# A final stage whose two accumulators are added on GpSimd instead of by accumulating DMAs

## What is computed

```python
hb = silu(xb @ exp_w1[e]) * (xb @ exp_w3[e])      # a block of 128 tokens, expert e
yb = hb @ exp_w2[e]
routed = segment_sum(yb * slot_w, slot_tok)        # add every block's rows to its tokens
y = routed + shared                                # shared: one expert that takes all tokens
x = x + g2 * y                                     # g2: one row for context, one for latents
out = x * rsqrt(mean(x * x) + EPS) * norm_final
```

## Time and profile before

| | us |
|---|---|
| median of 3 runs | 2050.85 (2050.64 to 2053.70) |
| the profiled execution | 2054.07 |
| its span in the trace | 2052.3 |
| PE busy in the span | 1856.0 (90%) |
| DVE busy | 1544.6 (75%) |
| ACT busy | 1306.6 (64%) |
| POOL busy | 753.4 (37%) |

### The profile page before, as it was taken

One profiled execution on the slowest core, in us unless ns is written; L12 is line 12 of the kernel. 1 busy time (PEld: TensorE's weight loads), 2 busy tenths in 40 slices (PEclk: granted clock), 3 DMA queues, 4 the chain that ended last, 5 costly groups with the idle time before them and its releaser, 6 DMA issues.

```text
span 2052.3 us, 34794 instructions
## 1 busy us (share of the span) xinstructions
PE 1856.0 (90%) x9251; PEld 1426.5 (70%) x9251; DVE 1544.6 (75%) x2092; ACT 1306.6 (64%) x1778; POOL 753.4 (37%) x754
## 2 busy tenths in 40 slices
PE   5787998999999899588999999999999999999960
PEld 2343444799898455466888888888888888888840
DVE  3366545442678578887999999999999999999956
ACT  3353545442324233457888888888888888888842
POOL 3211100000003114524354555565455556655532
PEclk8898999999999999689999999999999999999985
DMA  7833200235202323524786899886777878897977
GB/s 237 267 119 114 82 29 21 84 122 161 56 1 95 127 93 114 195 73 170 278 299 209 275 335 302 307 277 160 213 234 232 273 283 309 315 322 278 314 221 191
DMA packets 121260, 399.55 MB, mean 195 GB/s; under 512 B 28397, under 2 KB 52973, under 8 KB 96237
## 3 DMA queue, kind: packets, MB, share of 16 engines
q1 hardware_dynamic: 75644, 281.66, 37.2%
q0 software_dynamic: 45264, 117.06, 21.8%
q10 hardware_dynamic: 290, 0.02, 0.0%
HBM read 355.47 MB, written 84.60 MB: 214 GB/s over the span
## 4 chain that ended last, share of the span: by engine, by line
PE 48%; DVE 3%; issue 2%; DMA 2%; ACT 1%; POOL 1%; ACTq 1%; SPq 0%; DVEq 0%; POOLq 0%
PE bank L1977 28%; PE bank L1997 14%; PE bank L1964 5%; DMA y<-yacc_scratch 1%; PE bank L1984 1%; DVE wupl L2167 1%; ACT wuph L2074 1%; POOL slot_table L1906 1%; ACTq L1732 1%; DVE big L2282 1%; DVE big L2274 0%; DVE y L2273 0%; DMA xg<-hn_scratch 0%; DMA yacc_scratch<-y,idx_s 0%; ACT w2h L2083 0%
## 5 line engine op out<-in xcount | busy, mean ns | idle before, releaser
L2167 DVE TENSOR_TENSOR wupl<-big,wuph 128x2048 fp32r<-128x2048 f32 x230 | 526.5, 2290 | 83.8 <-ACT wuph L2074 79.3
L2074 ACT ACTIVATE wuph<-big 128x2048 fp32r (+1 forms) x230 | 439.5, 1912 | 14.9 <-issue 7.8
L1977 PE MATMUL bank<-wuph,xTh 128*128 128x512 f32 x912 | 366.6, 402 | 7.8 <-DVE xTl L2189 7.6
L1977 PE MATMUL bank<-wuph,xTl 128*128 128x512 f32 x912 | 358.3, 393 | 0.0
L1977 PE MATMUL bank<-wupl,xTh 128*128 128x512 f32 x912 | 357.1, 392 | 0.0
L1898 POOL DMA_INDIRECT yacc_scratch<-y,idx_s x105 | 230.3, 2193 | 285.6 <-ACT y L2065 262.6
L1888 POOL DMA_INDIRECT xg<-hn_scratch,idx_g x108 | 243.9, 2258 | 113.2 <-issue 109.4
L2175 DVE TENSOR_TENSOR w2l<-w,w2h 128x1024 fp32r<-128x1024 f32 x228 | 268.6, 1219 | 8.5 <-ACT w2h L2083 8.0
L2083 ACT ACTIVATE w2h<-w 128x1024 fp32r (+1 forms) x228 | 229.1, 1053 | 67.4 <-issue 58.8
L1997 PE MATMUL bank<-w2h,hT5h 128*128 128x512 f32 x456 | 191.4, 420 | 17.0 <-issue 7.9
L1977 PEld LDWEIGHTS bank<-wuph,xTh 128*128 128x128 f32 x912 | 172.5, 189 | 48.6 <-ACT wuph L2074 7.4
(11 more groups left out here) (360 smaller groups left out, 3162.6 us busy)
## 6 DMA issues: line engine op xcount, KB each, us to landing
big<-in_exp_w SPq DMA_DIRECT2D x128, 1024.0 KB, 9.9
w<-in_exp_w SPq DMA_DIRECT2D x64, 1024.0 KB, 11.7
wada<-in_w_ada POOLq DMA_DIRECT2D x16, 1024.0 KB, 6.1
wg<-in_w_in SPq DMA_DIRECT2D x14, 1024.0 KB, 5.4
wada<-in_w_ada SPq DMA_DIRECT2D x4, 2048.0 KB, 14.4
big<-in_w_in SPq DMA_DIRECT2D x8, 1024.0 KB, 5.5
yacc_scratch<-in_consts SPq DMA_DIRECT2D x9, 512.0 KB, 9.4
x<-x_scratch SPq DMA_DIRECT2D x9, 512.0 KB, 4.2
```

What stands on the lines that cost most here:

```text
L1977: mm = pe.matmul(b_up[j][:, :], x[:, k, :], w[:, :, k, :], start=(k == 0 and i == 0), stop=(k == KT - 1 and i == 2))
L2074: act.activation(part13(wup[j][0], half), raw13(e % WSLOT, half), ACT.Copy).then_inc(w_high, 1)
L2167: dve.tensor_tensor(part13(wup[j][1], half), raw13(e % WSLOT, half), part13(wup[j][0], half).bitcast(F32), ALU.subtract).then_inc(w_low, 1)
```

## The change

Line numbers in this section are those of the changed kernel where they stand in rows of it.

- Both accumulators are loaded plainly, by SP: `m.yacc[0]` into `y6`, then, after a wait for `y_out[1]`, `m.yacc[1]` into nine further tiles `y7`. Those lie over the first split up weights, the raw down weights `w2` (dead too) and the second split up weights. The four semaphores `s_y` now count both loads of a group.
- POOL adds `y7[t]` to `y6[t]` for tiles 1 to 8, with a TENSOR_TENSOR of 128x1024 each. DVE does the same for tile 0 itself.
- SP, not POOL, issues the nine stores.
- For the last block ACT calls `down_high` ahead of `ht`.

```diff
@@ SP, end of its program
             sp.wait_ge(y_out[0], n * 16 + 16 * ((NSH + 1) // 2))
+            for j, rows in enumerate((y6, y7)):
+                if j == 1:
+                    sp.wait_ge(y_out[1], n * 16 + 16 * ((NSH + 1) // 2))
+                for t in range(NT):
+                    sp.dma_start(rows[t][:, :], m.yacc[j][t * P:(t + 1) * P, :]).then_inc(s_y[batch_of(t)], 16)
             for t in range(NT):
-                sp.dma_start(y6[t][:, :], m.yacc[0][t * P:(t + 1) * P, :]).then_inc(s_y[min(batch_of(t), 1)], 16)
+                sp.wait_ge(y_new, t + 1)
+                dst = o[0][0] if t == 0 else o[1][0, (t - 1) * P:t * P, :]
+                sp.dma_start(dst, x3[t]).then_inc(s_out, 16)
+            sp.wait_ge(s_out, 16 * NT)
@@ POOL, end of its program
             for j, (t0, t1) in enumerate(YPARTS):
-                if j < 2:
-                    pool.wait_ge(s_y[j], 16 if j == 0 else 16 * (NT - 1))
+                pool.wait_ge(s_y[j], 32 * (t1 - t0))
                 for t in range(t0, t1):
-                    pool.dma_start(y6[t][:, :], m.yacc[1][t * P:(t + 1) * P, :], accum_op=ALU.add).then_inc(s_sum[j], 16)
-            for t in range(NT):
-                pool.wait_ge(y_new, t + 1)
-                dst = o[0][0] if t == 0 else o[1][0, (t - 1) * P:t * P, :]
-                pool.dma_start(dst, x3[t]).then_inc(s_out, 16)
-            pool.wait_ge(s_out, 16 * NT)
+                    if t >= 1:
+                        pool.tensor_tensor(y6[t][:, :], y6[t][:, :], y7[t][:, :], ALU.add).then_inc(s_sum, 1)
@@ ACT, last block
+            down_high(n * 2 + NSH, n * 2)
             ht(n * 2 + NSH)
-            down_high(n * 2 + NSH, n * 2)
@@ DVE
             def add(t):
-                t0, t1 = YPARTS[batch_of(t)]
-                dve.wait_ge(s_sum[batch_of(t)], 16 * (t1 - t0))
+                if t == 0:
+                    dve.wait_ge(s_y[0], 32)
+                    link(dve.tensor_tensor(y6[0][:, :], y6[0][:, :], y7[0][:, :], ALU.add))
+                else:
+                    dve.wait_ge(s_sum, t)
```

More of the change, by code:

```diff
@@ L1692, in stage_experts @@
         xg = m.xg
-        tail = lambda name, k: nc.alloc_sbuf_tensor_at(name, [P, D], F32, offset=at_wup[k // 8] + 4 * D * (k % 8))
-        x3, y6, sq6 = [m.late[:, t, :] for t in range(NT)], [tail(f"y6_{t}", t) for t in range(NT)], tail("sq6", NT)
+        room = [at + 4 * D * k for at, n in ((at_wup[0], 8 + 2 * WSLOT), (at_wup[1], 8)) for k in range(n)]
+        tail = lambda name, k: nc.alloc_sbuf_tensor_at(name, [P, D], F32, offset=room[k])
+        x3, y6, sq6 = [m.late[:, t, :] for t in range(NT)], [tail(f"y6_{t}", t) for t in range(NT)], tail("sq6", 2 * NT)
+        y7 = [tail(f"y7_{t}", NT + t) for t in range(NT)]
         gate6, nfrow = [m.late[:, NT + s, :] for s in range(2)], m.late[:, NT + 2, :]
@@ L1714, in stage_experts @@
         gathered = m.gathered
-        s_y, s_out = [sem(f"ld_y6_{j}") for j in range(2)], sem("st_y")
-        s_sum = [sem(f"sum_y6_{j}") for j in range(4)]
+        s_out, s_sum = sem("st_y"), sem("sum_y6")
+        s_y = [sem(f"ld_y6_{j}") for j in range(4)]
         x_new, x_sq, y_new, rooted = (sem(n) for n in ("x3_new", "x3_sq", "y_new", "rooted"))
@@ L1944, in _ @@
             hold(gathered[1], n * 16 + 16 * ((NSH + 4) // 2))
-            hold(y_out[1], n * 16 + 16 * ((NSH + 1) // 2))
+            pool.wait_ge(y_out[1], n * 16 + 16 * ((NSH + 1) // 2))
             for j, (t0, t1) in enumerate(YPARTS):
-                if j < 2:
-                    pool.wait_ge(s_y[j], 16 if j == 0 else 16 * (NT - 1))
+                pool.wait_ge(s_y[j], 32 * (t1 - t0))
                 for t in range(t0, t1):
-                    pool.dma_start(y6[t][:, :], m.yacc[1][t * P:(t + 1) * P, :], accum_op=ALU.add).then_inc(s_sum[j], 16)
-            for t in range(NT):
-                pool.wait_ge(y_new, t + 1)
-                dst = o[0][0] if t == 0 else o[1][0, (t - 1) * P:t * P, :]
-                pool.dma_start(dst, x3[t]).then_inc(s_out, 16)
-            pool.wait_ge(s_out, 16 * NT)
+                    if t >= 1:
+                        pool.tensor_tensor(y6[t][:, :], y6[t][:, :], y7[t][:, :], ALU.add).then_inc(s_sum, 1)
         @block.tensor
```

## The result

| | before | changed |
|---|---|---|
| median, us | 2050.91 (20 runs, 2046.75 to 2055.83) | 2056.32 (20 runs, 2054.41 to 2061.32) |
| profiled execution / its span | 2054.07 / 2052.3 | 2055.98 / 2054.2 |

The ratio is 1.0027, with a 95% interval of 1.0020 to 1.0034: 5.4 us slower (4.1 to 7.0). The direction is the forecast one, the size is about half of it.

What follows compares the result with a forecast made beforehand. The prediction took the final stage as bound by slow accumulating loads until 2020.4 us, then by DVE. Turns with POOL's adds +11.5, stores -0.3, down weights 0: +11.2 on 2050.85 gave 2062.0 us, range 2045.5 to 2068.

Steps and rivals of the forecast that it cites:

- The slow loads go: Final stage: without accumulating loads, `y7[0]` lands near 2004.8 us and DVE can start at 2004.9, not 2006.45.
- DVE's own work: Final stage: DVE's large instructions at 1.24 us each, with one more for tile 0, take 34.7 us together.
- What an add costs: One POOL add in the final stage takes 2.3 us, between 0.96 and 2.8; eight take 18.4 us.
- Behind `y7[0]` nothing can run beside anything: Final stage: DVE and POOL never overlap, so DVE's end is the sum 2004.9 + 34.7 + 18.4 = 2058.0 us.
- Turns in both directions: Final stage: DVE's two-SBUF-input instructions and POOL's adds block each other, making DVE end 11.5 us later.
- The hint of 25 ns: Before the change, DVE's L1362 took 717 ns beside POOL, 692 in the median: a hint that POOL stops DVE.
- Rival A: Final stage: DVE stops POOL, but POOL's adds don't stop DVE; faster, 2046.0 us; chance 0.20.
- B: Rival: exclusion holds but a POOL add costs one pass, 0.96 us; 2051.4 us; chance 0.14 with whatever lies between 2047 and 2055.
- C: Rival: a POOL add costs three full passes, 2.8 us; slower still, 2066.0 us; chance 0.12.
- The stores: End of the kernel: SP issues the last store sooner behind DVE, -0.3 us; the store's landing stays.
- Down weights first: Last block: PE's last matmuls start about 2.1 us sooner; counted as 0 at the end, bounds 0 to 1.5 us.
- the forecast's own case: DVE and POOL take turns with 2.3 us an add: 2056 to 2065 us, chance 0.54.

## Why the prediction was wrong in size

The path and the turns were right. Two terms of the sum were mis-sized: the stores, put at -0.3 us where the runs show -2.8, and the eight adds, put at 18.4 us of DVE's time where they took 16.2 to 16.5. Term by term:

**The slow loads go: right.** `y7` landed in time, DVE started at 29.2 us behind the marker where 2004.9 would be 29.7. No wait for a DMA came after.

**DVE's own work, 34.7 us: right.** It was 35.0 us with POOL's adds left out.

**What an add costs, 2.3 us: right for an add alone** (2.30 us), but the term of the sum was 8 x 2.3 = 18.4 us, and in turns it was 16.2 us (51.2 - 35.0). The step that failed here is "Behind `y7[0]` nothing can run beside anything": 0.24 us of each add does.

**Turns in both directions: right.** Each of seven DVE instructions took 1.9 to 2.2 us longer. The hint of 25 ns in the earlier trace rows may have been of the same kind; no run tests it, so it was thin evidence for the step that decided the sign. One count in the working was off: 29 copies of L1868, not 27, start inside an L2167, and 28 of them end 0.04 to 0.05 us behind it. The last one started 7 ns before that end and took 0.17 us, about its time alone. Rival A is out, and with it the lower end of the range. So are B's price for an add, 0.96 us, and C's, 2.8 us.

**The stores, -0.3 us: this is the term that was most wrong,** at -2.8 us. I priced the issue, 0.28 us, and stopped there. The span went on for 5.6 us from the last row on, the last store landed 3.3 us after its issue, and the DMA engines were idle in the last 2.3 us. That was to be seen before. Nor did "the store's landing stays" hold: with SP it came 0.65 us sooner after the issue.

**Down weights first, 0: not contradicted.** PE gained its 2.3 us, and SP's first load stayed at 11.2 us. But the last scatter came 2.2 us sooner, where I had given 1.5 us as the most. I had also overlooked that ACT's last copy waits for an older scatter of the same buffer. In the changed kernel it is that wait that releases it, not PE:

```profile
ACT y L2069 <- DMA yacc_scratch<-y,idx_s: 6.0, 1, 6.0
```

**The sum against the first profile of before:** start 2.0 us earlier rather than 1.5; work 51.2 rather than 53.1 us; end 2.8 rather than 0.3 us shorter. That takes 0.5 + 1.9 + 2.5 = 4.9 us from the forecast 11.2, and leaves 6.3; the tails give 83.5 - 77.1 = 6.4. That is inside the interval of the measured difference, 4.1 to 7.0 us.

**The last 1.0 us, to the measured 5.4,** is within the noise and needs no cause. The spread of the kernel before would give one of this size, though that is not shown: its first profile had the second earliest start of the eight accumulating loads, 29.6 us, against a mean of 30.8 over five profiles, of four different kernels. An estimate from that mean, 30.8 + 41.4 + 5.9, makes a tail of 78.1 us, and 83.5 - 78.1 = 5.4 us; that it meets the median to 0.1 us is luck. What is shown is that I took one profile's tail for the kernel's, and two profiles of it differ by 3.3 us.

The measured time of 2056.3 us lies inside the stated range, at the lower edge of what the forecast's own case had. The error is one of size: two terms that both gave too much, 2.5 and 1.9 us of 11.2.

## What to carry to other kernels

GpSimd is no second VectorE for elementwise work on SBUF where VectorE is busy with such work itself. While DVE runs instructions with two SBUF inputs, an add on POOL costs DVE 2.06 us and would cost 1.22 us on DVE itself; it shows in longer durations and hardly in waits. Look in the trace of before for one-element POOL instructions that end just behind a DVE instruction: they tell of one direction of it in advance. What POOL can give such a stage is DMAs that add on the way, for those tiles that are wanted late, with plain loads and DVE for the early ones. Where DVE ends the program, let SP issue the last stores and wait for them. Profile the kernel before twice when a few us matter.

## What I had not expected of the hardware

- A fill on POOL beside DVE's two-input instructions costs nothing (1.22 us for DVE, 0.95 us for the fill); the adds, which read, exclude them.
- A POOL add of 128x1024 is 2.30 us alone and takes 2.06 us of DVE's time in turns. A DVE instruction in turns ends 1.08 us behind the end of POOL's add.
- With stores that POOL issued and waited for, the program ended 5.9 us behind DVE's last instruction, 2.3 us of it with idle DMA engines; with SP's, 3.05 us. In the changed kernel, where POOL had eight adds ahead of its stores, it was 7.6 us, 4.0 of it with idle DMA engines.
- Plain loads by themselves ran at 414 GB/s, where plain loads mixed with a scatter had run at 345 and the accumulating loads at 180.
